# Gate/up differences remade partly on GpSimd, a changed product order, and other places for down's first weights

## The reference, cut to what matters

```python
x = x + rmsnorm(merged @ w_out, norm_mix_post)        # "out-projection", D = 1024
h2 = rmsnorm(x, norm_ffn_pre)
gate = h2 @ w_ffn_gate                                # 2048 x 1024 @ 1024 x 2816
up = h2 @ w_ffn_up
gp = jnp.pad(gate, ((0, 0), (1, 1), (0, 0)))
gate = gp[:, :-2] * conv_w[0] + gp[:, 1:-1] * conv_w[1] + gp[:, 2:] * conv_w[2] + conv_b
f = jax.nn.gelu(gate) * up
return x + rmsnorm(f @ w_ffn_down, norm_ffn_post)     # "down", 2048 x 2816 @ 2816 x 1024
```

## Time and profile before

| | |
|---|---|
| median of 3 runs | 2789.99 us (2786.79 to 2792.51) |
| the profiled execution | 2788.49 us, span 2786.8 us |
| mean granted TensorE clock | 0.983 of full speed |
| PE busy | 2664.8 us, 96% of the span |
| DVE busy | 1573.8 us, 56% |
| ACT busy | 921.2 us, 33% |
| GpSimd (POOL) busy | 860.5 us, 31% |
| PE waits for `u_two_three` (L1624) | 18.2 us in 2 waits |
| PE waits for splits of a (L1567) | 6.5 us in 5 |
| PE waits for splits of f (L1681) and of down's first weights (L1686) | 5.6 us in 3, 4.1 us in 3 |

### The profile page before, as it was taken

The page is one execution under the profiler, slowest core; times in us unless marked ns, Lnnn a source line. Parts: engine busy times, 40 slices in busy tenths (PEclk is TensorE's granted clock), DMA queues, the critical chain, the costliest instruction groups (busy, mean ns, idle before and its releaser), DMA issues.

```text
span 2786.8 us, 34638 instructions
## 1 busy us (share of the span) xinstructions
PE 2664.8 (96%) x12486; PEld 2189.9 (79%) x12486; DVE 1573.8 (56%) x2000; ACT 921.2 (33%) x1579; POOL 860.5 (31%) x1076
## 2 busy tenths in 40 slices
PE   7998999999999899999989999979999999999997
PEld 7886788788887677878868888868888877887886
DVE  5102674568799075454577766796777662224432
ACT  5221655622221160033453333343333341113221
POOL 2173330088785000012243344424443420001111
PEclk9999999999999999999999999989999999999999
DMA  6463225454626654554433222212222245335553
GB/s 221 94 256 75 70 70 159 137 178 133 191 92 204 122 206 166 212 153 147 146 103 129 84 90 83 84 60 83 84 82 78 83 147 149 103 102 175 164 166 109
DMA packets 367872, 361.77 MB, mean 130 GB/s; under 512 B 50672, under 2 KB 306672, under 8 KB 363504
## 3 DMA queue, kind: packets, MB, share of 16 engines
q1 hardware_dynamic: 311920, 266.47, 32.2%
q0 software_dynamic: 9856, 47.72, 5.1%
q10 hardware_dynamic: 45952, 45.67, 5.0%
HBM read 248.12 MB, written 111.67 MB: 129 GB/s over the span
## 4 chain that ended last, share of the span: by engine, by line
PE 48%; DVE 5%; issue 5%; DMA 4%; ACT 1%; POOL 1%; ACTq 0%; SPq 0%; POOLq 0%; DVEq 0%
PE tl_banks L406 9%; PE tl_banks L407 9%; PE tl_banks L408 9%; PE tl_banks L110 6%; PE tl_banks L112 6%; PE tl_banks L111 6%; DMA out<-dn_rows 2%; DMA dn_w_raw<-in_w_ffn_down 1%; DVE gu_b_lo L1573 1%; DMA dn_rows<-x_mid 1%; DVE dn_rows L475 1%; DVE dn_f_lo L1681 1%; PE tl_banks L1220 0%; DVE br_y_lo L787 0%; DVE gu_a_lo L1567 0%
## 5 line engine op out<-in xcount | busy, mean ns | idle before, releaser
L406 PE MATMUL tl_banks<-gu_b_hi,gu_a_hi 128*128 128x512 f32 x1232 | 483.7, 393 | 27.2 <-DVE gu_gate L1624 18.2
L407 PE MATMUL tl_banks<-gu_b_hi,gu_a_lo 128*128 128x512 f32 x1232 | 483.0, 392 | 0.0
L408 PE MATMUL tl_banks<-gu_b_lo,gu_a_hi 128*128 128x512 f32 x1232 | 482.9, 392 | 0.0
L406 PEld LDWEIGHTS tl_banks<-gu_b_hi,gu_a_hi 128*128 128x128 f32 x1232 | 233.4, 189 | 79.3 <-issue 21.9
L110 PE MATMUL tl_banks<-dn_w_hi,dn_f_hi 128*128 128x512 f32 x704 | 276.4, 393 | 11.1 <-DVE dn_f_lo L1681 5.6
L111 PE MATMUL tl_banks<-dn_w_hi,dn_f_lo 128*128 128x512 f32 x704 | 275.6, 392 | 0.0
L112 PE MATMUL tl_banks<-dn_w_lo,dn_f_hi 128*128 128x512 f32 x704 | 275.4, 391 | 0.0
L408 PEld LDWEIGHTS tl_banks<-gu_b_lo,gu_a_hi 128*128 128x128 f32 x1232 | 233.5, 190 | 49.0
L407 PEld LDWEIGHTS tl_banks<-gu_b_hi,gu_a_lo 128*128 128x128 f32 x1232 | 233.3, 189 | 48.4
L1567 DVE TENSOR_TENSOR gu_a_lo<-gu_raw,gu_a_hi 128x512 fp32r<-128x512 f32 x220 | 194.0, 882 | 99.6 <-ACT gu_a_hi L1374 99.6
L1374 ACT ACTIVATE gu_a_hi<-gu_raw 128x512 fp32r<-128x512 f32 x220 | 138.5, 630 | 245.4 <-PE tl_banks L408 237.3
(11 more groups left out here) (311 smaller groups left out, 5460.3 us busy)
## 6 DMA issues: line engine op xcount, KB each, us to landing
dn_f_raw<-f SPq DMA_DIRECT2D x64, 704.0 KB, 5.8
gu_raw<-in_w_ffn_gate SPq DMA_DIRECT2D x44, 512.0 KB, 3.8
gu_raw<-in_w_ffn_up SPq DMA_DIRECT2D x44, 512.0 KB, 3.8
gs_w_raw<-in_w_in SPq DMA_DIRECT2D x40, 512.0 KB, 4.5
gates<-gs_gate_out ACTq DMA_DIRECT2D x64, 256.0 KB, 2.8
br_rows<-gates POOLq DMA_DIRECT2D x16, 1024.0 KB, 7.0
f<-gu_conv SPq DMA_DIRECT2D x11, 1025.0 KB, 5.2
f<-gu_conv SPq DMA_DIRECT2D x11, 1023.0 KB, 5.7
```

The source lines that it names most:

```text
L406: pe.matmul(out, w_hi, x_hi, start=first, stop=False, skip_group_check=again)
L407: pe.matmul(out, w_lo, x_hi, start=False, stop=False, skip_group_check=again)
L408: return pe.matmul(out, w_hi, x_lo, start=False, stop=last, skip_group_check=again)
```

## The change

**Differences.** They get semaphores of their own. In pass 0, GpSimd makes a column difference and the fourth difference in tiles 9 to 14 of the out-projection loop, and DVE the first, third and second. In pass 1, GpSimd makes the first difference (behind the sums in unit 11), the third and the fourth (in unit 21), and DVE only the second; the operands stand in other places of `feat_raw`. The orders of ACT and DVE at the pass turn are written out as `turn_pass`; unit 22 runs its products in the order `SECOND`.

**Entry.** `finish_out(15)` moves behind the second differences on DVE, `u_two_three(0)` ahead of the last splits, the last `turn_tile` behind unit 0, its copy into ACT's unit 0. The last two late tiles go to `last_late`, and the wait for their store moves to the first convolution. In units 1 and 23 both convolutions and `u_two_three` come ahead of the splits.

**Down.** Raw weight pairs 1 to 10 are loaded to the place of their own low parts, each after a product of unit 43. Both halves of f tile 0 are split earlier, by way of `f_raw[0]`. The loads of f tile 2 are issued ahead of the last store.

```diff
-        mid_normed = place("ou_mid_normed", 202752, [P, 2, D])
+        mid_normed = place("ou_mid_normed", 202784, [P, 2, D])
+        last_late = place("ou_last_late", 202784, [P, 2, KD, P])
-        d_w_first = d_w_raw[0:2] + [place("dn_w_first2", 179200, [P, 2, BANK])]
+        d_w_lo_raw = place("dn_w_lo_raw", 90112, [P, KF, BANK])
         FIRST = (0, 4, 1, 2, 3, 5, 6)
+        SECOND = (0, 1, 3, 2, 4, 5, 6)
+        def b_source(p, j, k):
+            return feature(*{0: (k, 0), 1: (k, p), 2: (k, 1 - p), 3: (k, p), 4: (KHALF + k, 0), 5: (KHALF + k, 1),
+                             6: (KHALF + k, 0)}[j])
+        def first_weights(a):
+            return d_w_lo_raw[:, 2 * a:2 * a + 2] if a else d_w_raw[0][:]
-        EARLY_SPLITS = {6 + n: ((0, 4)[n // KHALF], n % KHALF) for n in range(2 * KHALF)}
+        EARLY_SPLITS = {5 + n: ((0, 4)[n // KHALF], n % KHALF) for n in range(2 * KHALF)}
+        EARLY_COLUMNS = {9 + k: k for k in range(KHALF)}
         EARLY_DIFFERENCES = {10 + k: k for k in range(KHALF)}
...
# SyncE
+            def load_first_tile():
+                load_f(0, 0, 0)
+                sync.wait_ge(f_lo_ready, 3)
+                sync.dma_start(f_raw[0][:], f_tiles[0, 1]).then_inc(f_in[1], 16)
+            def load_second_tile():
+                sync.wait_ge(f_lo_ready, 4)
+                sync.dma_start(f_raw[0][:], f_tiles[1, 0]).then_inc(f_in[0], 16)
+                sync.wait_ge(a_lo_ready, UNITS * OPS)
+                load_f(0, 1, 1)
             def load_first_weights(a):
-                if a in (1, 2):
-                    sync.wait_ge(product_done, nth(UNITS - 1, 0 if a == 1 else 3))
-                if a >= 3:
-                    sync.wait_ge(d_w_lo_ready, a - 2)
-                sync.dma_start(d_w_first[a % 3][:], w_pairs[0, a]).then_inc(d_w_first_in[a % 3], 16)
+                if a:
+                    sync.wait_ge(product_done, nth(UNITS - 1, 2 * a // KHALF))
+                sync.dma_start(first_weights(a), w_pairs[0, a]).then_inc(d_w_first_in[a], 16)
...
             load_first_weights(0)
+            load_first_tile()
             store(2 * PAIRS - 2)
-            sync.wait_ge(a_lo_ready, UNITS * OPS)
-            load_f(0, 0, 1)
             for a in range(1, 6):
                 load_first_weights(a)
-            load_tile(0, 1)
+            load_second_tile()
             for a in range(6, W_PAIRS):
                 load_first_weights(a)
+            load_tile(0, 2)
             store(2 * PAIRS - 1)
+            load_tile(0, 3)
             sync.wait_ge(f_stored, 2 * PAIRS * 16)
...
# GpSimd; column(k) waits for b_nth(0, 4, k), early_t_four(k) for column and T3
+            def second_t_one(k):
+                pool.wait_ge(late_in, KD * 16)
+                pool.tensor_tensor(feature(k, 1), feature(k, 1), feature(k, 0), ALU.subtract).then_inc(t_one_ready, 1)
+            def second_t_three(k):
+                pool.wait_ge(t_two_ready, KHALF + k + 1)
+                pool.tensor_tensor(feature(k, 0), feature(k, 1), feature(k, 0), ALU.subtract)\
+                    .then_inc(t_three_ready, 1)
+            def second_t_four(k):
+                pool.wait_ge(b_lo_ready, b_nth(1, 4, k))
+                pool.tensor_tensor(feature(KHALF + k, 0), feature(KHALF + k, 0), feature(k, 1), ALU.subtract)\
+                    .then_inc(t_four_ready, 1)
...
+                if u == PER_PASS // 2:
+                    for k in range(KHALF):
+                        second_t_one(k)
+                if u == PER_PASS - 1:
+                    for k in range(KHALF):
+                        second_t_three(k)
                 if u % 2:
                     times_up(u, 1, 1)
                     times_up(u, 0, 1)
                     up_edge(u)
+                    if u == PER_PASS - 1:
+                        for k in range(KHALF):
+                            second_t_four(k)
                     times_up(u, 1, 0)
...
# TensorE
-                if n == 4:
-                    turn_tile(TILES - 1)
+            turn_tile(TILES - 1)
             for u in range(1, UNITS):
-                for j in range(OPS):
+                for j in SECOND if u == PER_PASS else range(OPS):
                     product(u, j)
...
# VectorE, entry
             split_b(0, 1)
             split_a(0, 1)
-            finish_out(TILES - 1)
             split_b(0, 2)
             split_a(0, 2)
             for k in range(KHALF):
                 difference_two(0, k)
+            finish_out(TILES - 1)
+            split_a(0, 3)
             split_b(0, 3)
-            split_a(0, 3)
+            split_a(0, 5)
+            split_b(0, 5)
             norm_mid(TILES - 1)
-            split_b(0, 5)
-            split_a(0, 5)
-            for k in range(KHALF):
-                difference_four(0, k)
+            u_two_three(0)
+            split_a(0, 6)
             split_b(0, 6)
-            split_a(0, 6)
...
# VectorE, pass turn (ACT's turn_pass follows the same order of operands)
+            def turn_pass(u):
+                convolve(u, 0)
+                split_a(u + 1, 0)
+                split_b(1, 0)
+                convolve(u, 1)
+                split_a(u + 1, 1)
+                u_two_three(u)
+                split_b(1, 1)
+                for k in range(KHALF):
+                    difference_two(1, k)
+                c22(u)
+                c12(u)
+                c21(u)
+                split_a(u + 1, 3)
+                split_b(1, 3)
+                split_a(u + 1, 2)
+                split_b(1, 2)
+                split_a(u + 1, 4)
+                split_b(1, 4)
+                split_a(u + 1, 5)
+                split_b(1, 5)
+                u_two_three(u + 1)
+                split_a(u + 1, 6)
+                split_b(1, 6)
+                up_c11(u)
...
+                behind = u in (1, PER_PASS + 1)
+                if behind:
+                    convolve(u, 1)
+                    u_two_three(u)
...
# VectorE, last unit
             convolve(u, 0)
             convolve(u, 1)
-            split_f_lo(0, 0, [1])
-            split_first_weights_lo(0)
-            split_first_weights_lo(1)
+            for a in range(3):
+                split_first_weights_lo(a)
             u_two_three(u)
```

More of the change, by code:

```diff
@@ L923, in stage_tail @@
         dn = PostNorm(m, "dn", x_mid, ffn_post_gain, out, d_gain, d_rows, d_scaled, d_stat, d_consts)
-        d_w_first_in = [m.sem(f"dn_w_first_in{s}") for s in range(3)]
+        d_w_first_in = [m.sem(f"dn_w_first_in{a}") for a in range(W_PAIRS)]
         d_w_in = [m.pool_dma_sem(f"dn_w_in{s}") for s in range(3)]
@@ L1087, in _ @@
             dn.load_gain(sync)
-            with sync.Fori(2, TILES) as t:
+            with sync.Fori(4, TILES) as t:
                 load_tile(0, t)
@@ L1175, in _ @@
                     sum_two(0)
-            pool.wait_ge(turned, TILES)
+                if t in EARLY_COLUMNS:
+                    column(EARLY_COLUMNS[t])
+                if t - 1 in EARLY_DIFFERENCES:
+                    early_t_four(EARLY_DIFFERENCES[t - 1])
             pool.memset(gate[:, :, 0:1], 0.0).then_inc(edges_zero, 1)
@@ L1444, in norm @@
                 dn.scalar(act, t, s, [y_first[:, bass.ds(t, 1), :], banks[:, s, :]])
+            def turn_pass(u):
+                keep_one(u)
+                split_a(u + 1, 0)
+                split_b(1, 0, range(KHALF))
+                keep_five(u)
+                split_a(u + 1, 1)
+                split_b(1, 1, range(KHALF))
+                split_a(u + 1, 3)
+                gelu(u, 0)
+                gelu(u, 1)
+                split_b(1, 3, range(KHALF))
+                split_a(u + 1, 2)
+                split_b(1, 2, range(KHALF))
+                keep_one(u + 1)
+                split_a(u + 1, 4)
+                split_b(1, 4, range(KHALF))
+                keep_five(u + 1)
+                split_a(u + 1, 5)
+                split_b(1, 5, range(KHALF))
+                split_a(u + 1, 6)
+                split_b(1, 6, range(KHALF))
             act.sem_inc(d_y_done, 2)
@@ L1505, in _ @@
                         split_a(u + 1, j)
-                    if u == PER_PASS - 1:
-                        split_b(1, j, range(KHALF))
+                    if u == 0 and j == 1:
+                        keep_features(TILES - 1)
                     if u == UNITS - 1 and j < 6:
-                        if j == 0:
-                            split_f_hi(0, 0, [1])
                         if j in (3, 4):
                             gelu(u, j - 3)
-                        for a in range(2 * j, min(2 * j + 2, W_PAIRS)):
+                        for a in range(max(2 * j - 1, 0), 2 * j + 1):
                             split_first_weights_hi(a)
-                if u == UNITS - 2:
-                    split_f_hi(0, 0, [0])
+                if u in (UNITS - 3, UNITS - 2):
+                    split_first_f_hi(u - (UNITS - 3))
             act.wait_ge(product_done, UNITS * OPS)
@@ L1660, in convolve @@
                 p, pair, g = unit(u)
```

(37 more changed lines are left out.)

140 lines of the change are left out of this document (73 added, 67 removed).

## The result

The changed kernel takes 2760.8 us (median of 3 runs, 2757.7 to 2761.9) against 2790.0 (2786.8 to 2792.5): ratio 0.9894, 95% interval 0.9871 to 0.9916. The medians differ by 29.2 us; the two profiled executions show 27.7 of it, with a span of 2759.1 us against 2786.8.

What follows compares the result with a forecast made beforehand. TensorE is full between the joins, so only its stalls at entry, pass turn and down's start (53 us) can be won. 4.7 + 4.0 + 14.0 = 22.7 off the 2788.5 us execution gives 2765.8, median 2767; range 2756 to 2781.

Steps and rivals of the forecast that it cites:

- Start of down: Down's first tiles: early weight and tile loads remove the stalls, winning 14.0 of 14.2 us lost; lower bound 4.
- Moving the differences does not pay: Pass turn: giving eight differences to GpSimd loses 8.3 us in collisions and saves VectorE 4.8.
- The order pays: Pass turn: u_two_three of units 21 and 22 ahead of splits lets (21,6) start unhindered and unit 23 start earlier.
- Turn: Pass turn, units 21 to 24: unit 24 starts at 1890.3 instead of 1894.3, 4.0 us won.
- 15 x 1.04 = 15.6: Pass turn: VectorE loses 1.04 us to each of fifteen GpSimd operations, added to 34.4 of its own work.
- Wrong if T4 is what (22,6) waits for by more than 2 us: Failure sign at the pass turn: unit 22's product (22,6) held over 2 us by the fourth difference.
- The charge for a stall: TensorE at the joins: a stall over 2 us costs some 1.8 us more through the slow clock.
- Entry: From unit 0 to unit 2: unit 2 starts at 1449.5 instead of 1454.2, 4.7 us won.
- Full exclusion: Rival, chance 0.15: GpSimd operations cost VectorE their whole 1.29 us; entry and turn together bring about 1; 2775.
- Collisions beside PSUM operations: Rival, chance 0.12: collisions mostly fall beside PSUM operations and idle time; 8 + 9 + 14.2 = 31 won, 2759.
- Transfers: Rival, chance 0.10: transfers bound down's start, so only 4 us are won there; 2777.
- Starved GpSimd: Rival, slower, chance 0.04: GpSimd starved at the turn; gains gone at 4.6 us per operation; 2799 at 5.0.

Runs made afterwards that it cites:

- old_order: Changed kernel with u_two_three of units 21 and 22 at about their old places, third and fourth differences still on GpSimd; 2770.84 us, ratio 0.9933.
- t2_bank_early: Changed kernel with u_two_three of unit 22 ahead of the splits of operand five instead of behind them; 2760.90 us, ratio 0.9894.
- t34_left_out: Changed kernel with GpSimd's eight third and fourth differences of the second pass left out, only signals passed on; 2754.42 us, ratio 0.9874.
- t34_on_vector: Changed kernel with the eight third and fourth differences of the pass turn on VectorE instead of GpSimd; 2758.07 us, ratio 0.9887.
- finish_before_t2: Changed kernel with finish_out(15) ahead of the four second differences of the first pass instead of behind them; 2762.99 us, ratio 0.9902.

## Why the prediction was right, point by point

The time lies in the stated range, but 0.2 us below the forecast's own 2761 to 2773 and 6 below its 2767. Of the parts only down came as forecast; entry and turn brought 14.5 us, not 8.7.

- **Start of down, 14.0 forecast, 14.3 found.** All ten weight loads were issued from 2245.4 to 2259.7 (2258.8 to 2273.1 on the old clock, down's first tile being 13.4 earlier now; forecast to 2272.5), and the share was 0.96 at 309 GB/s in the 20 us named. No stall is left, and the transfers were no bound. Inside the part my picture was off: tile 2's own chain was worth 3.0, because most of the store's lateness went with the rest of the part.
- **Moving the differences does not pay: right for T3 and T4.** I had said 8.3 lost for 4.8 saved, 3.5. Put back on VectorE they win 2.9, and one of the eight costs VectorE 0.93 on average (1.04 forecast). What T1's move to unit 11 won was not tried by itself; it cost TensorE nothing (361.76 from unit 2 to 21 in both).
- **The order pays: right, and more than said.** old_order loses 10.5.
- **Turn, 4.0 forecast, 7.2 found.** The mis-sized term is "15 x 1.04 = 15.6": VectorE's stretch took 46.4 us against 34.4 of own work, 12.0. The price of a meeting was right, 1.07 for 1.04; the count was not. Of the fifteen operations one came later, three ran beside operations with an input in PSUM at no cost, and eleven were paid for. The same count fits the other kernels:

  | | before | changed | t2_bank_early | t34_left_out | t34_on_vector |
  |---|---|---|---|---|---|
  | VectorE's stretch, us | 48.2 | 46.4 | 47.5 | 39.0 | 43.9 |
  | its two-input operations lengthened to 1.4 us and more | 7 | 11 | 12 | 4 | 4 |
  | what these took above 0.68, us | 7.1 | 11.7 | 12.8 | 4.1 | 4.2 |

  b(1,6) was ready 48.6 us after unit 21's start instead of 52.2. "Wrong if T4 is what (22,6) waits for by more than 2 us" did come true, 2.85 us with GpSimd kept out for 6; but t2_bank_early and t34_left_out show that this wait is no term of its own. VectorE's sum holds with it.
- **The charge for a stall.** The row behind "1.8 us on top" was misread: from 1842.18 to 1847.41 run the 12 matmuls of one product, not 15, so 5.2 us stood for 2.7 of work, 2.5 lost. And not every stall over 2 us pays it (below). Where VectorE sets the pace it costs nothing more: the product (22,6) takes 6.64 to 6.66 us in six kernels, at granted clocks from 0.53 to 0.76.
- **Entry, 4.7 forecast, 7.3 found.** Unit 1 started 8.8 earlier, not 7.8: (0,6) began 26.0 after unit 0 and not 26.6, and took 3.6 with the turned tile and not 4.2. And (1,6) waited 1.11, not 1.6, with no slow clock behind it, where I had charged 1.5. The stall before (0,2) was too long in the forecast as well, but is no part of this sum (finish_before_t2): (0,2) came 13.72 us after unit 0, 0.95 later than before and not 2.0, after 4.0 us of wait and not near 5. Its bank is free after the 1.4 us that read it (L470), not after all 2.6 of finish_out.
- **Rivals.** Full exclusion: refuted in the size, since it charged all fifteen with 1.29 and eleven paid 1.07. The Trainium skill (SBUF — State Buffer, section Who interferes with whom) says that such pairs block each other fully. Where two operations meet, this trace comes near to that: T2 and T3 alternate every 1.70 us, where VectorE's takes 0.60 of the time and GpSimd's 1.29 when undisturbed, 1.89 together. Collisions beside PSUM operations: partly, for three of fourteen, and it is this rival that the time came nearest to (2759), with 7.3 and 7.2 where it had 8 and 9. (Its 9 for the turn does not follow from the 19 operations that gave the minus 1 of full exclusion: 4.0 and 19 x 0.44 are 12.) The Trainium skill's rule in the same section, that a VectorE instruction with at most one SBUF input, outside certain faster modes, does not contend, agrees with the sum at 1823.37, 1.30 us beside VectorE's undisturbed 0.68, and with T4's first result behind the bank sums, twice. Transfers, no change: refuted. Starved GpSimd: it happened to one operation (6.0 us, over the 4.6 of the turning point), but not to all eight; the four T3 averaged 1.70 and the four T4 2.62.

What stays open: why GpSimd takes turns with VectorE in T3 (1.7 us each) and is kept out by VectorE at T4's start. Both meet operations with two SBUF inputs. The runs show what ends the exclusion (a PSUM operation, a pause of VectorE), not what starts it.

## What to carry to other kernels

Cut two traces at the same matmuls and forecast stretch by stretch: three of the eight stretches here agree within 0.03 us before and after, and four others carry the whole gain. Offloading from VectorE to GpSimd has to be priced with what each operation takes from VectorE as well as with what it saves; at 0.93 against 0.6 the order of the work was the gain and the offload of T3 and T4 a loss. The price falls only where two such operations meet, so count the meetings, and put operations with an input in PSUM beside the other engine's work. A wait taken out of one product of a chain that another engine sets comes back at a later one (2.4 us saved before (0,2), 1.9 more before (0,3) and 1.3 before (0,6)), and the clock behind it can be the slow one there.
